# Last projection with tokens on the partitions: residual opened in PSUM, final norm rooted per partition

## What is computed

```python
h = h + mixed @ w_out[i]
f = rmsnorm_2(h, norm_ffn_g[i])
h = h + (jax.nn.silu(f @ w_gate[i]) * (f @ w_up[i])) @ w_down[i]
out = rmsnorm_2(h, norm_final_g)          # mean of squares over the 1024 features, then the gain
return out[:, N_META:]                    # the 256 real tokens
```

## Time and profile before

| | |
|---|---|
| three runs | 1436.81, 1437.00 and 1440.79 us; median 1437.0 us |
| the profiled execution | 1439.02 us, of which the span shown in the profile is 1437.0 us |
| TensorE busy | 1241.8 us, 86% of the span |
| VectorE busy | 873.5 us, 61% |
| ScalarE busy | 638.8 us, 44% |
| mean granted TensorE clock | 0.976 |

### The profile page before, as it was taken

How to read it: one execution, slowest core, us unless ns; L and a number is a source line. 1 busy time by engine, 2 the same in 40 slices (tenths; PEclk the granted TensorE clock), 3 DMA queues, 4 the chain that set the end, 5 groups by cost and what they waited for, 6 DMA issues and landing times.

```text
span 1437.0 us, 19477 instructions
## 1 busy us (share of the span) xinstructions
PE 1241.8 (86%) x6652; PEld 877.5 (61%) x6652; DVE 873.5 (61%) x1847; ACT 638.8 (44%) x1420; POOL 265.3 (18%) x300
## 2 busy tenths in 40 slices
PE   6999887787777878787777877999999989899996
PEld 4888774232222223332222325999999989899996
DVE  6743567666666667776666545467745556554455
ACT  4654443444444344544444334244435563434443
POOL 4000004333333333333333330000000020000000
PEclk9999999999999999999999999999999999999998
DMA  5321338999999999999999992345533345455551
GB/s 215 132 89 60 107 115 349 421 422 421 422 421 421 421 422 420 389 423 421 422 421 421 422 422 104 103 161 175 176 121 130 104 155 169 140 181 177 177 187 58
DMA packets 66919, 377.75 MB, mean 263 GB/s; under 512 B 7440, under 2 KB 7568, under 8 KB 33952
## 3 DMA queue, kind: packets, MB, share of 16 engines
q0 software_dynamic: 36864, 268.45, 45.0%
q1 hardware_dynamic: 29840, 107.85, 22.7%
q10 hardware_dynamic: 144, 0.56, 0.1%
HBM read 375.78 MB, written 1.05 MB: 262 GB/s over the span
## 4 chain that ended last, share of the span: by engine, by line
PE 54%; DMA 31%; DVE 5%; ACT 5%; issue 4%; DVEq 0%; SPq 0%; ACTq 0%
DMA work<-in_rows,work 31%; PE ps L502 30%; PE ps L800 7%; PE ps L859 4%; PE ps L537 2%; PE ps L540 1%; PE ps L543 1%; ACT work L1202 1%; DVE w_lo L333 1%; DVE work L1446 1%; ACT work L1198 1%; ACT w_hi L325 1%; DVE work L1451 1%; PE ps L940 1%; PE ps L730 1%
## 5 line engine op out<-in xcount | busy, mean ns | idle before, releaser
L800 PE MATMUL ps<-work 128*128 128x512 f32 x1024 | 507.4, 626 | 138.9 <-ACT work L1202 138.9
L800 PEld LDWEIGHTS ps<-work 128*128 128x128 f32 x1024 | 180.8, 193 | 461.9 <-ACT work L1202 315.0
L1780 DVE CUSTOM_DVE_ANT_0 work<-work,ps 128x1024 f32<-128x1024 f32 x256 | 312.4, 1220 | 219.4 <-DMA work<-in_rows,work 219.3
L454 POOL DMA_INDIRECT work<-in_rows,work x256 | 241.1, 942 | 601.3 <-PE ps L800 387.8
L333 DVE TENSOR_TENSOR w_lo<-ring,w_hi 128x1024 fp32r<-128x1024 f32 x198 | 242.6, 1230 | 152.1 <-ACT w_hi L325 150.7
L502 PE MATMUL ps<-x_hi,w_hi 128*128 128x256 f32 (+1 forms) x1248 | 318.0, 295 | 12.6 <-ACT x_hi L343 7.2
L502 PE MATMUL ps<-x_lo,w_hi 128*128 128x256 f32 (+1 forms) x1248 | 308.3, 287 | 0.0
L502 PEld LDWEIGHTS ps<-x_hi,w_hi 128*128 128x128 f32 x1248 | 238.4, 194 | 19.7 <-issue 11.2
L502 PEld LDWEIGHTS ps<-x_lo,w_hi 128*128 128x128 f32 x1248 | 236.7, 193 | 0.3
L325 ACT ACTIVATE w_hi<-ring 128x1024 fp32r<-128x1024 f32 x198 | 205.5, 1052 | 60.7 <-PE ps L859 28.6
L1195 ACT ACTIVATE work<-work 128x1 f32<-128x1 f32 x256 | 51.9, 203 | 350.3 <-DVE work L1780 348.8
(11 more groups left out here) (275 smaller groups left out, 1086.5 us busy)
## 6 DMA issues: line engine op xcount, KB each, us to landing
ring<-in_stream SPq DMA_DIRECT2D x198, 512.0 KB, 3.3
work<-in_rows,work POOLq DMA_INDIRECT x256, 15.3
res<-in_tokens SPq DMA_DIRECT2D x4, 272.0 KB, 3.5
gain_rows<-in_gain_rows SPq DMA_DIRECT2D x1, 1024.0 KB, 9.5
out_dram<-work SPq DMA_DIRECT2D x2, 512.0 KB, 2.7
work<-in_kiwi ACTq DMA_DIRECT2D x1, 544.0 KB, 3.5
work<-in_keys SPq DMA_DIRECT2D x1, 512.0 KB, 8.7
small<-in_small SPq DMA_DIRECT2D x1, 225.0 KB, 5.4
```

Of the source, the lines that this page charges most:

```text
L454: g.indirect_dma_start(out=gathered[:, n % ROWS, :], out_offset=None, in_=rows_dram, in_offset=bass.IndirectOffsetOnAxis(ap=expert[:, n:n ...
L800: last = mm(ps[:, Y_BANK[t] + j, :], diag[:, n % DIAGS, :], gathered[:, n % ROWS, D + 512 * j:D + 512 * j + 512], start=False, stop=k == S ...
L1780: v.tensor_tensor_reduce(R["product"][:, D * (n % 2):D * (n % 2) + D], gathered[:, n % ROWS, 0:D], ps[:, bank:bank + 2, :].rearrange("p b ...
```

## The change

The last projection is turned over: now the hidden tile (`x_hi`, `x_lo`) is the weight operand, 128 tokens at a time, and the row block of `w_down` is the moving operand with 512 columns. Tokens come to lie on the partitions. `row_tile` makes one block for one half of the tokens with 3 parts x 2 column halves = 6 matmuls, so a block has 12 of 512 columns. Banks 4 and 5 hold tokens 0 to 127, banks 6 and 7 tokens 128 to 255. The last two blocks are done for the first half of the tokens and then for the second.

The sums are opened with the residual: 16 float32 matmuls with a 128x128 piece of `res` as weight and the identity as moving operand. Twelve of them stand before the sum of `norm(2)` and four behind it; the zero matmuls are gone, and so are `close_sums` and `add_sums`. `norm(2)` now sums in bank 2.

The final norm reads PSUM: per half of the tokens one ACT square of 128x1024 with a running sum over the row, a logarithm and an exponential of 128x1, then two DVE operations of 128x512 that multiply by the root of the partition and by the gain. The gain comes as a 512 KB array by a new DMA on ACT's queue ahead of the gate/up stage. ACT loads the table set for logarithm and exponential ahead of the first row block. The output is stored in four DMAs of 256 KB.

```diff
@@ pe
-            def open_sums():
-                for n in range(4):
-                    mm(ps[:, 4 + n, :], zeros[:, :], res[:, 0:2, 0:REAL], start=True, stop=True)
...
+            def open_sums(chunks):
+
+                for c in chunks:
+                    tile_is_taken(pe, TILE0["w_out_2"] + c)
+                    for t in range(2):
+                        mm(ps[:, 4 + 2 * t + c // 4, P * (c % 4):P * (c % 4) + P],
+                           res[:, c, META + P * t:META + P * t + P], ident[:, :], start=c % 4 == 0, stop=True,
+                           skip_group_check=True)
+
+            def row_tile(b, t, turn=0, n=0):
 
                 parts_ready(b, turn)
                 pe.wait_ge(x_lo_ready, turn * RING + (n + 1))
                 k = b % RING
...
+                at = k * REAL + P * t
+                first = None
+                for x, w in ((x_hi, w_hi), (x_hi, w_lo), (x_lo, w_hi)):
+                    for j in range(2):
+                        last = mm(ps[:, 4 + 2 * t + j, :], x[:, at:at + P], w[:, k, 512 * j:512 * j + 512],
+                                  start=False, stop=True, skip_group_check=True)
+                        first = last if first is None else first
+                return first, last
...
+            open_sums(range(0, 6))
             norm(2, REAL)
+            open_sums(range(6, 8))
             columns("w_gate_up_2", REAL, X_FFN)
-            open_sums()
             b0, turns = FIRST["w_down_2"], FF // RING
             with pe.Fori(0, turns) as i:
                 for k in range(RING):
-                    row_block(b0 + k, i, HIDDEN0 + k)
-            for k in range(turns * RING, FF):
-                row_block(b0 + k, 0, HIDDEN0 + k)
-            close_sums()
-            norm(3, REAL)
+                    first, _ = row_tile(b0 + k, 0, i, HIDDEN0 + k)
+                    first.then_inc(block_begun, 1)
+                    row_tile(b0 + k, 1, i, HIDDEN0 + k)
+            for t in range(2):
+                for k in range(turns * RING, FF):
+                    _, last = row_tile(b0 + k, t, 0, HIDDEN0 + k)
+                last.then_inc(down_ready, 1)
@@ scalar
+            act.dma_start(ffa["gain"], gain_dram).then_inc(gain_landed, 16)
             gate_tiles()
...
             tiles_are_taken(act, g0 + 2 * FF)
+            nc.scalar.preload_act_table_set("natural_log_exp_and_others")
             b0 = FIRST["w_down_2"]
...
-            for piece in range(4):
-                act.wait_ge(residual, 4 + piece + 1)
-                square(res[:, :, META:], sq_r, piece)
-            root(3)
+            for t in range(2):
+                act.wait_ge(down_ready, t + 1)
+                a(final_sq[:, t, :, :], ps[:, 4 + 2 * t:6 + 2 * t, :], ACT.Square,
+                  accum_out=final_sum[:, t:t + 1]).then_inc(final_step, 1)
+                act.wait_ge(final_step, 2 * t + 1)
+                a(final_rstd[:, t:t + 1], final_sum[:, t:t + 1], ACT.Ln, scale=1.0 / D,
+                  bias=eps[:, 0:1]).then_inc(final_step, 1)
+                act.wait_ge(final_step, 2 * t + 2)
+                a(final_rstd[:, t:t + 1], final_rstd[:, t:t + 1], ACT.Exp, scale=-0.5).then_inc(final_rooted, 1)
@@ vector
-            add_sums(1)
-            dve.wait_ge(residual, 8)
-            norm(3, res[:, :, META:], "norm_final", outT, tokens_of(sq_late, REAL))
+            dve.wait_ge(gain_landed, 16)
+            for t in range(2):
+                dve.wait_ge(final_rooted, t + 1)
+                for j in range(2):
+                    part = slice(512 * j, 512 * j + 512)
+                    stt(out_tok[:, t, part], ps[:, 4 + 2 * t + j, :], final_rstd[:, t:t + 1], ffa["gain"][:, part],
+                        ALU.mult, ALU.mult).then_inc(out_ready, 1)
@@ sync
-            for half in range(2):
-                sp.wait_ge(normed, 2 * 3 + half + 1)
-                part = slice(half * 4 * REAL, (half + 1) * 4 * REAL)
-                sp.dma_start(out_dram[:, part], outT.rearrange("p c t -> p (c t)")[:, part]).then_inc(stored, 16)
-            sp.wait_ge(stored, 32)
+            for n in range(4):
+                sp.wait_ge(out_ready, n + 1)
+                part = slice(512 * n, 512 * n + 512)
+                sp.dma_start(out_dram[:, part], ffa["out"][:, part]).then_inc(stored, 16)
+            sp.wait_ge(stored, 64)
```

More of the change, by code:

```diff
@@ L87 @@
 for _name, _n in (("glr", C * GLA_RANK), ("gate_up", GLA_HEADS * GLA_DK), ("norm1", C), ("norm2", C),
[L88 removed]
+                  ("norm_ffn", C), ("sb_norm", 4),
                   ("gla_norm", 4), ("b_gate", 2), ("conv", CONV_K * C)):
@@ L117, with build @@
 OWN = (0, 5, 10, 15, 20, 26, 32)
-def build(nc, stream, rows_dram, small_dram, keys_dram, kiwi_dram, x_dram, gain_rows_dram, meta_2_dram, out_dram):
+def build(nc, stream, rows_dram, small_dram, keys_dram, kiwi_dram, gain_dram, x_dram, gain_rows_dram, meta_2_dram, out_dram):
     with ExitStack() as ctx:
@@ L309, in build @@
         vis_ready = sem("vis_ready")
+        gain_landed, down_ready, final_step, final_rooted, out_ready = (
+            sem(n) for n in ("gain_landed", "down_ready", "final_step", "final_rooted", "out_ready"))
         X_MIX = 2
@@ L370, in norm_bank @@
         def norm_bank(k):
-            return 2 if k == 3 else 7
+            return 2 if k == 2 else 7
         def bank_of(g):
@@ L855, in row_block @@
                 k = b % RING
[L856 to L864, removed]
-                mm(ps[:, 7, 0:1], zeros[:, :], ones[:, 0:1], start=False, stop=True,
-                   skip_group_check=True).then_inc(y_ready, 1)
+                at = k * REAL + P * t
[6 more added lines that the diff above has]
+                return first, last
             pe.wait_ge(early_hi, 3)
@@ L1877, in _ @@
                     part_lo(0, slice(0, META), early_hi, 3, early_lo)
-            def add_sums(n):
-                dve.wait_ge(y_ready, n)
-                for m in range(4):
-                    r = res[:, 2 * m:2 * m + 2, META:]
-                    tt(r, r, ps[:, 4 + m, :].rearrange("p (c t) -> p c t", c=2), ALU.add).then_inc(residual, 1)
             scale_sums(1)
@@ L2089 @@
               "kiwi": np.ascontiguousarray(features(np.concatenate([ki, ki, wi], axis=1))),
+              "gain": np.ascontiguousarray(np.broadcast_to(a["norm_final_g_2"], (P, D))),
               "gain_rows": np.ascontiguousarray(np.broadcast_to(
@@ L2098 @@
     out = nc.dram_tensor("out_dram", (P, C * REAL), F32, kind="ExternalOutput").ap()
-    build(nc, dram["stream"], dram["rows"], dram["small"], dram["keys"], dram["kiwi"], dram["tokens"], dram["gain_rows"], dram["meta_2"], out)
+    build(nc, dram["stream"], dram["rows"], dram["small"], dram["keys"], dram["kiwi"], dram["gain"], dram["tokens"], dram["gain_rows"], dram["meta_2"], out)
     r = run_bass_kernel_spmd(nc, [{f"in_{k}": v for k, v in arrays.items()}], core_ids=[0])
     got = r.results[0]["out_dram"]
-    return np.ascontiguousarray(got.reshape(P, C, REAL).transpose(2, 1, 0)).reshape(1, REAL, D)
+    return np.ascontiguousarray(got.reshape(P, 2, D).transpose(1, 0, 2)).reshape(1, REAL, D)
```

11 lines of the change are left out of this document (5 added, 6 removed).

## The result

The changed kernel takes 1428.8 us (median of 5 runs, 1425.6 to 1429.0) against 1437.4 us before (5 runs, 1436.8 to 1441.4). The ratio is 0.9926, with a 95% interval of 0.9909 to 0.9942. So it is faster, by 0.6% to 0.9%, inside the predicted range (1422 to 1431 us) and 2.4 us above the predicted time of 1426.4 us.

A forecast was written before the change was run, and what follows sets the result against it. TensorE's work and waits were taken to bound the kernel, with 13.4 us behind the last row product. Terms -0.5 + 0.8 + 2.0 - 6.3 - 7.6 = -11.6 us gave 1427.4 or 1425.4, middle 1426.4 us; range 1422 to 1431.

The forecast's parts named there:

- term 4: Row stage: 264 matmuls of 512 columns replace 528 of 256, stepping in 0.216 us; 57.0 us, -6.3 us.
- term 1: Gap of norm(2): identity matmuls shorten TensorE's idle time, so less low clock in the gate/up stage; -0.5 us.
- term 3: Clock at the junction before the row stage: falls after 4.4 us of TensorE idle, slowing row matmuls; +2.0 us.
- term 5: Tail from last row matmul to end of span: 5.8 us in place of 13.4; -7.6 us.
- term 2: Junction before the row stage: table load ahead of split and x_hi delays the first row matmul; +0.8 us.
- the forecast's own range: Whole kernel: 1423.5 to 1429.5 us, from the bounds of terms 1, 3, 4 and 5.
- the cost per matmul stays: Rival, row stage: 512-column matmuls step in 0.2265 us, 2.8 us less gain, 1429.2 us; chance 0.17.
- My own sign of being wrong: Row stage: the prediction is wrong if the row matmul step is over 0.23 us.
- bound by the splitting: Rival, row stage: splitting, not TensorE, keeps it at 2.88 us a block; term 4 zero, 1432.7 us; chance 0.07.
- The clock outlasted neither gap: Rival, norm(2) and junction: clock falls at neither; terms 1 and 3 become -1.7 and 0, 1423.2 us; chance 0.06.
- The drain: Rival, junction: the table load brings a drain there, +1.4 us, 1427.8 us; chance 0.04.

The follow-up runs named there:

- zero_cover: Changed kernel plus four zero float32 matmuls of 512 columns on TensorE between gate/up and row stage; 1427.2 us, 0.9926 to before.
- load_late: Changed kernel with the logarithm table load moved from ahead of the first row block to behind the row stage's last x_hi; 1426.9 us, 0.9925 to before.
- sums_behind: Changed kernel with all 16 identity matmuls behind the sum of norm(2); 1429.3 us, 0.9939 to before.
- all_covered_2: Changed kernel with late table load, three zero matmuls behind the last identity matmuls and three behind the gate/up stage; 1425.7 us, 0.9915 to before.
- two_stores: Changed kernel with the output stored in two DMAs of 512 KB in place of four of 256 KB; profiled only, tail 6.2 us against 6.0.
- both_moved: Changed kernel with the table load behind the row stage's last x_hi and all 16 identity matmuls behind norm(2)'s sum; 1426.0 us, 0.9921 to before.
- both_covered: Changed kernel with late table load, all 16 identity matmuls behind norm(2)'s sum and three zero matmuls at the junction; 1425.3 us, 0.9899 to before.

## Why the prediction was right, and where it was not

The direction, the range and the order of the terms held. The sum was too large: 11.6 us forecast, 7.0 and 8.2 us measured in the two pairs of profiles for the stretch that the terms speak of, and 8.6 us between the medians. That the first pair of spans differs by 10.7 us, so close to the sum, is luck: 3.7 of it lie ahead of the change. The 4.6 us by which the sum misses the first pair are term 4 (3.1), term 1 (1.1), term 3 (0.5) and term 5 (0.2), less 0.3 of term 2. The time still lies inside the forecast's own range, near its upper end of 1429.5, because the bounds of the terms together are as wide as the miss.

**Term 4 is the step that failed** ("The two nearest rows by width both say that the extra is hidden under a stream this long, so I take 0.216"). The step is 0.2267 us; the rival "the cost per matmul stays", given 0.17 and 1429.2 us, describes what happened. Measured at the full clock the stage takes 60.2 us, so it gives 3.2 us in place of 6.3. My own sign of being wrong, a step of over 0.23 us, could not tell the forecast from this rival. I had two rows for the hidden extra, and neither was about width. The matmuls at the low clock show no extra at any width: 512 columns there step in 0.43 us, which is 512 at 1.2 GHz with nothing on top, and 256 in 0.214, while at the full clock both show it. And the zero matmuls are float32, whose records take twice their columns and almost nothing more (0.429 us at 512 columns, 0.112 at 128). The 0.216 itself stands in neither row; they gave 0.2145. The row that counted was the earlier trace rows: 0.012 us at 272 columns, equal to that at 256. The Trainium skill, "TensorE: Matmul & The Clock Gate", section Wait — 56ns, not 53.3ns?, says the same in kind: a fixed cost per matmul that shows only at the high clock. Its size of 2.5 ns would give 0.216 us; the runs here show 13 ns for fp32r operands and 12 for bfloat16 read with a stride, and they decide. Only the float32 records, 2 ns over their columns, come near the page.

**Term 3** (+2.0) was right in kind and close in size: 2.45 us by zero_cover, and 1.6 to 2.8 us over all profiles with this wait. The wait was 3.95 us, not 4.4. (The 2.4 to 5.8 us that its working gives for the low clock are not 2 us either way of "over 4"; the measured 5.3 lies in them all the same.) **Term 2** (+0.8) measured +0.5, the value that I had named for a load that runs over the 0.34 us behind L2007. load_late puts the load's share at 1.05 us. There is no drain behind it: the split starts 0.01 us after the load ends.

**Term 1** (-0.5) measured +0.6 in the first pair and -0.6 in the second (129.6 to 129.0 us), so nothing on average: both kernels show both values. The clock fell there with the shorter idle time too, in each of the seven profiles that have this order and no cover at norm(2). The sum came 0.1 us later behind `w_out_2`, not 0.3, and the cover for it held. That the gain was there to be had, 1.4 to 2.1 us of it, is shown by sums_behind and all_covered_2.

**Term 5** (-7.6) measured -7.4. Its working had one wrong part, what the smaller last store is worth (0.65 us forecast, 0.2 shown by two_stores). DVE's two operations took 0.1 us more than counted, and the root was ready 0.2 us sooner, half of that by the exponential's 0.20 us. The sum of 5.8 us became 6.0.

**The rivals.** The row stage is not bound by the splitting: ACT still waits 1.35 us for TensorE in each period, and the period of 2.72 us is TensorE's 12 steps. The clock outlasted neither gap. The drain did not appear.

## What to carry to other kernels

Turning a product over so that it has half as many, twice as wide matmuls saved a fixed 13 ns per start and nothing else: 3.2 us, of which the low clock at the junction took 2.5 back. The large gain was to have one number per token on its own partition, so that the final norm needs no sum over partitions and reads the open sums directly. Ask of each wait that a change uncovers how long TensorE is idle in it: here 4 us of waiting cost 1.6 to 2.8 us more in the stage behind, and matmuls that add zero took that away, in the profiles, at no cost of their own. Put a table load where its engine waits anyway, not behind the wait that opens a stage.

## What the runs showed of the hardware

- A matmul with fp32r operands steps in its columns plus 0.0133 us at the full clock, at 256 and at 512 columns (0.120 and 0.2267 us), and so nearly with bfloat16 operands read with a stride (0.225 us for 512). In all of these each matmul has a weight load of its own in the trace, also where the weight is the same as before. At the low clock the extra is gone (0.214 and 0.43 us). Float32 records do not show it (0.429 us, twice the 0.2133 us of 512 columns and 0.002 more).
- After the same idle stretch of 2.4 us ahead of the sum the clock stayed at 1.00 in sums_behind and fell in both_moved and both_covered. After 2.9 us at the junction it stayed up in load_late and fell in both_moved. After 3.4 us and more at these two places it fell each time.
- The clock also falls with TensorE busy by the trace. In the first profile of before, it fell while the matmuls of 8 columns at 902 us ran (0.82 on average from 902 to 906), and the 272-column matmuls behind them ran at 0.50:

```profile
902.03 4.53 PE L886 MATMUL ps<-work 128*128 128x8 f32 x32
```

```profile
906.00:911.00 5.00, 5.00 (x23) 5.00 (x24) 0.00 (x0) 0.47 (x2) 0.00 (x0) 0.50 0.00 0
```

In the profile of after the same place runs at 1.00. The thousand matmuls from the first of these on take 131.1 us in the first profile of before and 128.0 in its second, where the clock does not fall here. Such places are where executions of one kernel differ by about 3 us.
